# Seven products for three instead of two of the eight row-block pairs of the gate/up matrices, with the chunk loops unrolled

## The reference, cut to what matters

```
def swiglu_ffn(x, norm_g, w_gate, w_up, w_down):
    h = rms_norm(x, norm_g)                                # x: 256 x 2048
    return (jax.nn.silu(h @ w_gate) * (h @ w_up)) @ w_down # w_gate, w_up: 2048 x 5632

layer 0:  x += chunked_sgu_mixer(x);  x += swiglu_ffn(x)
shared keys and values from x
layer 1:  x += moba_attention(x);     x += swiglu_ffn(x)
```

## Time and profile before

| | |
|---|---|
| median of 3 runs | 2124.43 us (2124.36 to 2124.97) |
| the profiled execution: time | 2123.94 us |
| its span | 2121.8 us |
| busy: PE, DVE, ACT, POOL | 2110.1, 1415.5, 1079.8, 35.7 us |
| matmuls | 9638 |
| chain that ended last, by engine | PE 97%, DVE 2%, ACT 1% |
| bytes read from HBM | 399.56 MB, 189 GB/s |

### The profile page before, as it was taken

One profiled execution on the slowest core, in us unless ns is written; L12 is line 12 of the kernel. 1 busy time (PEld: TensorE's weight loads), 2 busy tenths in 40 slices (PEclk: granted clock), 3 DMA queues, 4 the chain that ended last, 5 costly groups with the idle time before them and its releaser, 6 DMA issues.

```text
span 2121.8 us, 25577 instructions
## 1 busy us (share of the span) xinstructions
PE 2110.1 (99%) x9638; PEld 1751.7 (83%) x9638; DVE 1415.5 (67%) x1553; ACT 1079.8 (51%) x1308; POOL 35.7 (2%) x47
## 2 busy tenths in 40 slices
PE   9999999999999999999999999999999999999999
PEld 7888878888888888888888888878888888888887
DVE  5466577775677578855556565577874677578754
ACT  6443555553444345545566565465553444355532
POOL 1000000000000000000000001000000000000000
PEclk9999999999999999999999999999999999999999
DMA  8655546555655556655555444546555655566653
GB/s 326 209 177 169 175 164 229 178 198 189 213 194 178 198 187 207 201 177 180 197 179 171 165 162 162 172 159 224 171 198 198 215 182 178 198 198 199 210 171 134
DMA packets 202625, 402.80 MB, mean 190 GB/s; under 512 B 7120, under 2 KB 7728, under 8 KB 202288
## 3 DMA queue, kind: packets, MB, share of 16 engines
q1 hardware_dynamic: 201760, 398.49, 56.5%
q0 software_dynamic: 784, 3.19, 0.4%
HBM read 399.56 MB, written 2.10 MB: 189 GB/s over the span
## 4 chain that ended last, share of the span: by engine, by line
PE 97%; DVE 2%; ACT 1%; DMA 0%; issue 0%; SPq 0%; ACTq 0%
PE acc L1252 17%; PE acc L1256 17%; PE acc L1254 17%; PE acc L1393 13%; PE acc L1395 13%; PE acc L1394 13%; PE tr L1300 2%; PE tr L1394 1%; PE tr L1393 1%; PE tr L1395 1%; DVE w_lo L830 0%; DMA raw<-in_a_w_in_dram 0%; DVE a_lo L856 0%; PE tr L1363 0%; PE tr L1515 0%; PE tr L1525 0%
## 5 line engine op out<-in xcount | busy, mean ns | idle before, releaser
L830 DVE TENSOR_TENSOR w_lo<-raw,w_hi 128x1024 fp32r<-128x1024 f32 x567 | 685.0, 1222 | 441.3 <-ACT w_hi L476 440.7
L476 ACT ACTIVATE w_hi<-raw 128x1024 fp32r<-128x1024 f32 x567 | 597.4, 1060 | 674.5 <-PE acc L1256 359.3
L1393 PE MATMUL acc<-w_hi,a_hi 128*128 128x512 f32 x1056 | 412.7, 391 | 3.4 <-DVE w_lo L830 3.4
L1395 PE MATMUL acc<-w_hi,a_lo 128*128 128x512 f32 x1056 | 411.1, 389 | 0.0
L1394 PE MATMUL acc<-w_lo,a_hi 128*128 128x512 f32 x1056 | 410.8, 389 | 0.0
L1252 PE MATMUL acc<-w_hi,h_hi 128*128 128x512 f32 x696 | 271.6, 390 | 0.0
L1256 PE MATMUL acc<-w_hi,h_lo 128*128 128x512 f32 x696 | 270.9, 389 | 0.0
L1254 PE MATMUL acc<-w_lo,h_hi 128*128 128x512 f32 x696 | 270.8, 389 | 0.0
L1252 PE MATMUL acc<-w_hi,a_hi 128*128 128x512 f32 x640 | 255.1, 399 | 0.8 <-DVE a_lo L856 0.5
L1256 PE MATMUL acc<-w_hi,a_lo 128*128 128x512 f32 x640 | 249.8, 390 | 0.0
L1254 PE MATMUL acc<-w_lo,a_hi 128*128 128x512 f32 x640 | 249.4, 390 | 0.0
(11 more groups left out here) (187 smaller groups left out, 2262.6 us busy)
## 6 DMA issues: line engine op xcount, KB each, us to landing
raw<-in_ffn_w_down_dram SPq DMA_DIRECT2D x88, 1024.0 KB, 5.1
raw<-in_ffn_w_gate_dram SPq DMA_DIRECT2D x66, 1024.0 KB, 5.1
raw<-in_ffn_w_up_dram SPq DMA_DIRECT2D x66, 1024.0 KB, 5.1
raw<-in_a_w_in_dram SPq DMA_DIRECT2D x30, 1024.0 KB, 5.5
raw<-in_ffn_w_gate_dram SPq DMA_DIRECT2D x44, 512.0 KB, 3.7
raw<-in_ffn_w_up_dram SPq DMA_DIRECT2D x44, 512.0 KB, 4.5
raw<-in_a_w_out_dram SPq DMA_DIRECT2D x16, 1024.0 KB, 5.1
raw<-in_w_v_dram SPq DMA_DIRECT2D x16, 1024.0 KB, 5.1
```

Source lines behind the costliest of these rows:

```text
L476: nc.scalar.activation(dst, src, ACT.Copy).then_inc(hi_split, 1)
L830: nc.vector.tensor_tensor(lo, src, hi, ALU.subtract).then_inc(lo_split, 1)
L1393: nc.tensor.matmul(bank[:, :], hi, rhs_hi, start=start, stop=False)
L1395: return nc.tensor.matmul(bank[:, :], lo, rhs_hi, start=False, stop=stop)
```

## The change

WINO becomes 3: chunks with c > 0 have three pairs by seven products and ten half groups. Their order is g3 g4 g5 g6 s0 g7 u7 s1 u3 u4 s2 u5 u6: the first pair stands behind four half groups, and two half groups stand between two pairs. The first chunk of each layer keeps its order and its two pairs. All chunk loops are unrolled; the tables of half groups, pairs, loads and slots are made when the program is built. The rings go by the half group's number (`m % RING`), and raw slots are taken in turn (load number mod 4), each load waiting for what last read its slot. The load `g7 u7` takes its halves from both matrices, with two DMAs of 512 KB.

Hooks move: `gate_sums` and `read_p1` stand after g4, `hidden` and `silu` after g5, the transposes after g4 (the second half group; in `down` after the second too, where a part of four chunks had them after the third). The sums of s0 follow g6's split directly, and pair_lo of s0 follows them; the sums of s1 and s2 stand likewise directly before their low parts. In the first chunk of a layer the sums of s0 stand after u2, ahead of u3's split and of the last activations' low part. PE's wait for `h_lo` (which frees `tr`) moves from before the first pair to its middle, before its products into `tr`. `forms` is made for three pairs: the operands grow from 1024 to 1536 columns, the four small ones from 256 to 384, and the first sum goes to a buffer of its own, `form_a`, that lies over `s_lo`.

```diff
-    WINO = 2
+    WINO = 3
+    ORDER_1 = items("g2 g3 g4 g5 u2 u3 g6 s0 g7 u4 u5 s1 u6 u7")
+    LOADS_1 = [items(w) for w in ("g2 g3", "g4 g5", "u2 u3", "g6 g7", "s0", "u4 u5", "s1", "u6 u7")]
+    ORDER_N = items("g3 g4 g5 g6 s0 g7 u7 s1 u3 u4 s2 u5 u6")
+    LOADS_N = [items(w) for w in ("g3 g4", "g5 g6", "s0", "g7 u7", "s1", "u3 u4", "s2", "u5 u6")]
...
-            def forms():
+            def forms(layer):
+                a = form_a
+                if layer:
+                    dve.wait_ge(s_used, 3 * (LAST_PAIR[layer - 1, NF - 1] + 1))
+                step.inc(nc.vector.tensor_tensor(a[:, :, :].rearrange("p a c -> p (a c)"),
...
+                        if c == 0:
+                            hooks = {("g", 2): [lambda: forms(layer)], ("g", 4): [lambda: forms_lo_part(layer)],
+                                     ("g", 5): [first_hooks[0][0]], ("u", 2): [lambda: sums(c, 0)],
+                                     ("u", 3): [first_hooks[0][1]], ("u", 4): [lambda: sums(c, 1)]}
+                        else:
+                            hooks = {("g", 6): [lambda: sums(c, 0)], ("u", 7): [lambda: sums(c, 1)],
+                                     ("u", 4): [lambda: sums(c, 2)]}
+                            if c > c0:
+                                hooks[("g", 4)] = [lambda: gate_sums(c - 1)]
+                                hooks[("g", 5)] = [lambda: hidden(c - 1, CHUNK_END[layer, c - 1])]
+                                hooks[("g", 6)].insert(0, lambda: dve.wait_ge(staged, b0 + c - NC))
+                                hooks[("s", 0)] = [lambda: hidden_lo(c - 1, c0)]
+                            else:
+                                hooks[("g", 6)].insert(0, first_hooks[p][0])
...
                 products(acc[0][1], block(o, 1), *t4, start=False, stop=last).then_inc(s_used, 1)
+                if tr_read is not None:
+                    pe.wait_ge(lhs_lo, tr_read)
                 products(tr[0], form(s1), *t1, start=first, stop=last)
...
-                    chunk(0, True, p == 0)
-                    with pe.Fori(1, c1 - c0) as i:
-                        chunk(i, False)
+                    for c in range(c0, c1):
...
-                    unit(base, h_hi, h_lo, 0, {2 if n > 6 else 1: [lambda: transpose_batch(b0 + c1 - 1)]},
-                         {0: b0 + c1 - 1, n - 2: b0 + c1}, n=n)
+                    unit(base, h_hi, h_lo, 0, {1: [lambda: transpose_batch(b0 + c1 - 1)]},
+                         {0: b0 + c1 - 1, n - 2: b0 + c1}, j0=base, n=n)
```

## The result

The changed kernel took 2111.07 us (median, 2110.51 to 2111.55), the kernel before 2124.39 us beside it (2124.09 to 2124.97): a ratio of 0.9937 (95% interval 0.9921 to 0.9952), 13.3 us faster. 2110.8 was forecast. The profiled execution took 2110.95 us with a span of 2108.8 (2123.94 and 2121.8 before, so 13.0 us of span).

A forecast was written before the change was run, and what follows sets the result against it. PE was taken as the bound, the steady loop worth exactly its count of matmuls. 2123.94 us profiled - 13.6 (60 fewer matmuls) + 0 (all other terms) = 2110.3, plus 0.5 for the median: 2110.8 us; range 2107.8 to 2117.5.

The forecast's parts named there:

- The count: Gate/up chunks after each layer's first: third pair saves 60 matmuls in all, 13.6 us; period falls to 42.37 us.
- The third pair on DVE: Steady chunk: DVE gets 4.3 us more, 38.7 of 42.4 us, but no pair is late; 0 us of waiting.
- rival B: DVE slightly late by whole durations plus hand-overs; PE waits 0.3 us in 16 chunks; 2117 us; chance 0.11.
- the spare at s0: Steady chunk's first pair: DVE's low parts done about 16.1, PE can begin at 17.20; 1.1 us spare.
- rival C: DVE becomes the bound at s0 and s1; about 2142 us, slower from 2.0 us on; chance 0.07.
- ACT's casts: Steady chunk: ACT's casts from the sums finish before DVE's low parts ask, covered by 0.7 us at s0.
- Unrolling: Unrolled chunk loops: no time at the jump back on PE, so 0 us, bounds -1 and +1.
- Part starts: Four first chunks of parts 1 and 2: s0 ready at +10.4, PE wants it at 10.88; 0 us, bounds 0 and 0.5 each.
- First chunks of the layers: Larger forms +2.0 us, sums pulled ahead; layer 0's s0 1.9 us sooner, layer 1's 2.0 later; together 0, bounds -2, +3.
- The sum: Whole kernel: 2123.94 - 13.6 + 0 = 2110.3 us profiled, 0.5 more for the median, 2110.8 us.
- T1: Theory before the experiments: time is PE's count plus first-pair waits in layers' first chunks; DVE hidden elsewhere, about a microsecond spare.
- T2: Opposing theory: DVE or longer code partly eats the third pair's gain; unrolling and moved sums make up for it.

The follow-up runs named there:

- e1: Changed kernel with two pairs a chunk instead of three, the old order, and forms for two pairs: 2121.45 us.
- e4: Changed kernel plus one unused DVE instruction of 1024 columns ahead of the first pair in 16 steady chunks: 2116.09 us.
- e8: Changed kernel with a fourth pair a chunk (WINO = 4), one half group between pairs: 2178.76 us.
- e3: Changed kernel with the sums of s0 in each layer's first chunk back behind u3's split and the last activations' low part: 2113.02 us.
- e5: Changed kernel with ACT saving the last residual after its casts of u2 and u3 in each layer's first chunk, not before them: 2106.61 us.
- e7: Changed kernel plus two unused DVE instructions ahead of the first pair in 16 steady chunks: 2133.59 us.
- e2: Changed kernel with the third pair's forms made after u6 in each layer's first chunk, those of two pairs where they were: 2108.15 us.
- e6: Changed kernel with both the third pair's forms made late and the residual saved after the casts of u2 and u3: 2105.12 us.

## Why the prediction held, step by step

**The count.** 9578 matmuls, period 42.37: exact, and e1 shows that all of the 0.68 us a chunk is the third pair's. 20 x 0.68 = 13.6.

**The third pair on DVE.** Forecast positions, each from the end of s2 on PE (the matmul after it starts at 369.87), against the rows above: g6 +8.37, measured 8.33; sums +9.50, measured 9.47; end of the low parts +16.03, measured 16.08 (385.95); end of those of s1 +26.0, measured 26.07 (394.72 + 1.22). DVE 38.7 of 42.4, measured 38.35. Adding the measured spacings of 25 instructions gave each of them to 0.1 us. That also settles rival B: by whole durations they would lie a microsecond later. The Trainium skill (VectorE: DVE Perf Modes, The DRAIN you can't avoid) has the next operation start when the pipeline is empty, but the same section adds that a next operation that is not held starts earlier, which the forecast left out when it set the page against the trace. Here the sums start 1.14 us after a split of 1.22 us (378.20, 379.34), so they are of the second kind, and the chain is to be summed by spacings.

**The term that was mis-sized** is the spare at s0. The forecast compared the end of the low parts with the start of the matmul and got 1.1 us; e4 showed that the load is what has to be met: 0.9. With it rival C's turning point moves from 2.0 to about 1.6 us of further work on DVE ahead of s0. It cost the forecast nothing, as 0.9 was enough. The wait on PE is 0 per chunk, as taken.

**ACT's casts** were early, as forecast, at s0 and s1. At s2 they weren't: DVE waits 0.32 us for one. The step had looked only at PE's end of s1 plus the casts and named no number for DVE's asking; what holds DVE is the first cast, which starts at 399.60, when PE is through the first third of s1. The spare at s2 (2.4 us) hid it. e8 shows what becomes of it when that spare is gone.

**Unrolling** was taken at 0 with bounds of 1: e1 confirms 0 in the loop. The changed kernel fetches 1.15 MB of instructions on queue q8 where the kernel before had 0.90, without a visible cost there. One thing may belong here, though. In the attention loop, which the change doesn't touch, one gap is new:

```profile
1140.78 0.39 PE L1255 MATMUL acc<-w_hi,a_lo 128*128 128x512 f32 x1
...
1141.35 0.50 PE L1251 MATMUL acc<-w_hi,a_hi 128*128 128x512 f32 x1 [0.18 <-DVE w_lo L831]
```

0.57 us from start to start, 0.34 over the spacing. e3, e4, e5 and e7 have it too; the kernel before, e1, e2, e6 and e8 don't. It goes neither with the number of pairs, nor with the amount of instructions (e1 and e2 fetch the same 1.15 MB), nor with any edit near it. That it comes from where the code lies in memory is a guess that no run tested: it stays open, with some 0.4 us.

**Part starts.** No gap, as taken: DVE is done 0.46 us ahead of the pair's first matmul, 0.48 by the forecast. To the first load it is only 0.23 us, the narrowest of all pairs that start on time; the forecast, which summed to the matmul, didn't see that.

**First chunks of the layers.** Layer 0: s0 sooner by 1.9, forecast 1.9; e3 undoes it and loses 1.95. Layer 1: later by 2.0, forecast 2.0; e2 undoes it. That the two cancel was right for the reasons given: the moved sums fill DVE's idle time in layer 0, in layer 1 there is none behind u2's split (the idle 3.44 us lies ahead of it, and e5 uses it), and the larger forms are on the chain in layer 1. The rows of the forms are 1.75 and 0.56 us as forecast from the slopes:

```profile
1390.77 1.75 DVE L866 TENSOR_TENSOR form_a<-a_hi,a_lo 128x1536 f32<-128x1536 f32 x1
1392.55 0.56 DVE L872 TENSOR_TENSOR sums_b<-form_a 128x384 f32<-128x384 f32 x1
```

What the forecast didn't see is that they needn't cost anything: the third pair isn't in the first chunk, so its forms could wait (e2).

**The sum.** -13.6 (count) - 1.9 (layer 0) + 2.0 (layer 1) + 0.4 (the gap, open) = -13.1, measured -13.0 of span and -13.3 of the medians. That the forecast of the median is only 0.3 us off is in part luck: the profiled execution was put at 2110.3 and took 2110.95, mostly the gap; the 0.5 added from there to the median was 0.1 this time. T1 stands; of T2 nothing is left in the steady chunks.

## What to carry to other kernels

Where an engine is at its count of instructions, a saving is worth exactly its count as long as the engine that pays for it meets each of its deadlines; sum that engine by the spacings of its own rows, position by position, since its busy share (91% was free, 92% of e8 was not) doesn't tell. For TensorE measure the spare to the weight load of the first matmul, a matmul earlier. After such a change look for what was made larger ahead of its need: the larger forms here cost 0.8 and 1.9 us at the two layer starts, where the third pair wasn't used yet, and mending that and one order of casts gave another 6 us (2105.12).

## What the runs showed of the hardware

A weight load that has to wait for its data costs PE 0.25 us even when the data come just in time for the matmul (e4). It then starts 0.11 us after DVE's end. Data that come 0.23 us ahead of the load cost nothing (part starts of the change, s1 in e4).

TensorE's granted clock fell for a moment in e3, e4 and e7, each time in layer 1's first chunk. In e3 it fell after waits of 0.58 (1398.11) and 1.99 us (1409.45); windows of e3 (stretch, length, busy us of PE, PEld, DVE, ACT, POOL, clock, DMA share, GB/s):

```profile
1400.00:1409.00 9.00, 7.47 (x37) 6.01 (x36) 5.56 (x6) 4.62 (x9) 0.00 (x0) 1.00 0.64 224
1409.00:1414.00 5.00, 4.55 (x13) 3.66 (x14) 4.97 (x9) 3.77 (x6) 0.89 (x2) 0.66 0.47 143
1414.00:1420.00 6.00, 5.55 (x26) 4.27 (x24) 5.97 (x7) 4.85 (x5) 0.00 (x0) 1.00 0.14 56
```

The mean of 0.66 is made of matmuls at the lower of the two levels, 1.2 GHz, started 0.43 us apart, and others at 2.4 GHz. It cost nothing, as PE waited for DVE right after it: from layer 1's first gate/up matmul to the pair it took 25.3 us in e3 and 25.2 in the change. The waits don't decide it alone: e4 has waits of 0.57 and 2.00 us there and a clock of 0.66 in the 5 us after the second, e7 0.57 and 2.02, with 0.50 in the stretch from 1420.13 to 1421.63; in the change, with 0.55 and 2.01, the clock stayed at 1.00. What tells them apart is open.
